# Attention scores from high and low parts: two products of 128 filled rows in place of three half-empty ones

## The reference, cut to what matters

```python
def _dilated_branch_prompt(q, k, v, window, dil):
    ...
    s = jnp.einsum('brcqhd,brckhd->brchqk', qb, kw).astype(F32) * (HEAD_DIM ** -0.5)
    ...
    p, lse = _masked_softmax(s, valid[None, None, :, None])
    o = jnp.einsum('brchqk,brckhd->brcqhd', p, vw.astype(F32))

def _combine(outs, lses):
    w = jax.nn.softmax(jnp.stack(lses, axis=0), axis=0)
    return jnp.sum(w[..., None] * jnp.stack(outs, axis=0), axis=0)
```

## Time and profile before

| | |
|---|---|
| time, median of 3 runs | 1917.29 us (1916.12 to 1919.46) |
| time of the profiled execution | 1917.52 us |
| its span, first to last instruction | 1915.7 us |
| mean granted TensorE clock | 0.937 |
| PE busy | 1698.6 us (89%) |
| DVE / ACT / POOL busy | 832.1 / 562.3 / 554.9 us |

### The profile page before, as it was taken

The page is one execution under the profiler, slowest core; times in us unless marked ns, Lnnn a source line. Parts: engine busy times, 40 slices in busy tenths (PEclk is TensorE's granted clock), DMA queues, the critical chain, the costliest instruction groups (busy, mean ns, idle before and its releaser), DMA issues. The chain is left out here.

```text
span 1915.7 us, 22177 instructions
## 1 busy us (share of the span) xinstructions
PE 1698.6 (89%) x8272; PEld 1373.3 (72%) x8272; DVE 832.1 (43%) x1552; ACT 562.3 (29%) x828; POOL 554.9 (29%) x265
## 2 busy tenths in 40 slices
PE   6999999979898688876699689999999999999983
PEld 3778888857676566655588568787878788878862
DVE  4632212046465345566556223333333333333489
ACT  4322222225555155542344221111111111111121
POOL 0233333343000035585000232222222222222354
PEclk9999999979899589986799899999999999999997
DMA  8554433451100667763142211111111111111132
GB/s 290 203 178 155 171 124 121 160 142 56 56 0 24 177 201 219 221 205 111 65 149 80 67 44 44 44 44 44 44 44 44 44 44 44 44 44 44 44 88 93
DMA packets 137588, 192.19 MB, mean 100 GB/s; under 512 B 10034, under 2 KB 86882, under 8 KB 137387
## 3 DMA queue, kind: packets, MB, share of 16 engines
q1 hardware_dynamic: 125396, 168.83, 27.9%
q10 hardware_dynamic: 12128, 22.55, 3.2%
HBM read 162.42 MB, written 28.93 MB: 100 GB/s over the span
## 5 line engine op out<-in xcount | busy, mean ns | idle before, releaser
L2420 POOL TENSOR_TENSOR mlp_w_lo<-w_room,mlp_w_hi 128x2048 fp32r<-128x2048 f32 x31 | 143.7, 4637 | 320.6 <-ACT mlp_w_hi L2416 320.5
L2721 PE MATMUL ps<-mix_hi,mlp_w_hi 128*128 128x512 f32 x512 | 206.4, 403 | 15.1 <-DVE mlp_w_lo L2420 9.6
L2619 DVE TENSOR_TENSOR x<-x,ps 128x512 f32<-128x512 f32 x224 | 154.1, 688 | 141.9 <-PE ps L2792 141.2
L2598 DVE TENSOR_TENSOR mlp_h_lo<-mlp_pos,mlp_h_hi 128x512 fp32r<-128x512 f32 x64 | 69.3, 1083 | 332.8 <-ACT mlp_h_hi L2522 330.7
L2721 PE MATMUL ps<-mix_hi,mlp_w_lo 128*128 128x512 f32 x512 | 203.2, 397 | 0.0
L2721 PE MATMUL ps<-mix_lo,mlp_w_hi 128*128 128x512 f32 x512 | 202.8, 396 | 0.0
L584 POOL TENSOR_TENSOR inp_a_lo<-inp_room,inp_a_hi 128x2048 fp32r<-128x2048 f32 x24 | 111.6, 4649 | 273.8 <-ACT inp_a_hi L718 273.8
L2792 PE MATMUL ps<-mlp_w_hi,mlp_h_hi 128*128 128x512 f32 x448 | 175.8, 392 | 5.5 <-PE ps L2727 5.1
L2792 PE MATMUL ps<-mlp_w_hi,mlp_h_lo 128*128 128x512 f32 x448 | 174.5, 389 | 0.0
L2792 PE MATMUL ps<-mlp_w_lo,mlp_h_hi 128*128 128x512 f32 x448 | 174.3, 389 | 0.0
L637 PE MATMUL ps<-inp_whi,z_hi 128*128 128x512 f32 x384 | 150.3, 391 | 2.4 <-PE ps L637 1.3
(11 more groups left out here) (375 smaller groups left out, 3512.8 us busy)
## 6 DMA issues: line engine op xcount, KB each, us to landing
w_room<-in_w_ff SPq DMA_DIRECT2D x32, 1024.0 KB, 7.0
inp_room<-in_w_ada SPq DMA_DIRECT2D x16, 1024.0 KB
proj<-inp_row ACTq DMA_DIRECT2D x54, 256.0 KB, 2.5
x<-in_cache_k SPq DMA_DIRECT2D x48, 256.0 KB, 5.0
cache_V<-in_cache_v SPq DMA_DIRECT2D x48, 256.0 KB, 4.8
x<-in_x_prompt SPq DMA_DIRECT2D x16, 512.0 KB, 9.5
inp_room<-in_w_ada_f SPq DMA_DIRECT2D x8, 1024.0 KB
x<-in_w_in ACTq DMA_DIRECT2D x16, 512.0 KB, 6.7
```

Source lines behind the costliest of these rows:

```text
L2420: pool.tensor_tensor(lo, raw, hi.bitcast(F32), ALU.subtract).then_inc(ready, 1)
L2598: dve.tensor_tensor(h_lo[s][:, j, cols], pos[u % 2][:], h_hi[s][:, j, cols].bitcast(F32), ALU.subtract).then_inc(h_ready, 1)
L2619: dve.tensor_tensor(dst, dst, ps[:, 5 + o % 3, :], ALU.add).then_inc(added, 1)
L2721: mm = pe.matmul(ps[:, u, :], w[:, k, j * P:(j + 1) * P], z[:, k, rows], start=(k == 0 and a == 0), stop=(k == KT - 1 and a == 2))
```

## The change

The keys get one tile for each head, `k_both[h]`: in the head's own 64 rows the high part, in the other 64 rows the low part. The queries keep `q_hi[h]` with zeros in the other rows and get `q_both[h]`: the low part in the own rows and a copy of the high part in the other rows. Then `q_hi x k_both` is high x high, and `q_both x k_both` is low x high + high x low in one sum over 128 rows: two products for every 512 columns instead of three.

ACT makes the high keys in two instructions of 64 rows in place of one of 128, and copies the high queries to the other rows, two new instructions of 64 rows each (`moved`). DVE makes the low keys in two instructions of 64 rows, written to the other rows. Two of the four memsets are left. ACT no longer waits for the memsets; PE does, once, and waits for the first move before `scores(0)`, for the second before unit 8.

```diff
         q_hi = [st.sb(f"qhi{h}", [P, S], F32R) for h in range(2)]
-        q_lo = [st.sb(f"qlo{h}", [P, S], F32R) for h in range(2)]
-        k_hi, k_lo = st.sb("khi", [P, S], F32R), st.sb("klo", [P, S], F32R)
+        q_both = [st.sb(f"qboth{h}", [P, S], F32R) for h in range(2)]
+        k_both = [st.sb(f"kboth{h}", [P, S], F32R) for h in range(2)]
+        OWN = [slice(HD * h, HD * (h + 1)) for h in range(2)]
+        OTHER = OWN[::-1]
...
                         if u >= 2:
                             pe.wait_ge(scored, base + u - 1)
+                        if u == TT:
+                            pe.wait_ge(moved, 2 * (2 * i + s) + 2)
...
-                            for a, (x, y) in enumerate(((q_hi, k_hi), (q_hi, k_lo), (q_lo, k_hi))):
-                                mm = pe.matmul(out, x[h][:, q * P:(q + 1) * P], y[:, c:e], start=(a == 0), stop=(a == 2))
+                            at = slice(q * P, (q + 1) * P)
+                            pe.matmul(out, q_hi[h][:, at], k_both[h][:, c:e], start=True, stop=False)
+                            mm = pe.matmul(out, q_both[h][:, at], k_both[h][:, c:e], start=False, stop=True)
...
-                    pe.wait_ge(split_done, 3 * (2 * i + s) + 3)
+                    pe.wait_ge(zeroed, 2)
+                    pe.wait_ge(split_done, 4 * (2 * i + s) + 4)
+                    pe.wait_ge(moved, 2 * (2 * i + s) + 1)
...
         def _(act):
-            act.wait_ge(zeroed, 4)
...
                     def take_keys(s):
                         act.wait_ge(turned, 2 * (2 * i + s) + 2)
-                        act.copy(k_hi[:], banks(ps, 2, 2)).then_inc(hi_done, 1)
+                        for h in range(2):
+                            act.copy(k_both[h][OWN[h], :], banks(ps, 2, 2)[OWN[h], :]).then_inc(k_hi_done, 1)
+                        for h in range(2):
+                            act.wait_ge(q_hi_done, 2 * (2 * i + s) + h + 1)
+                            act.copy(q_both[h][OTHER[h], :], q_hi[h][OWN[h], :].bitcast(F32)).then_inc(moved, 1)
...
         def _(dve):
-            for x in (q_hi, q_lo):
-                for h in range(2):
-                    rows = slice(HD * (1 - h), HD * (2 - h))
-                    dve.memset(x[h][rows, :].bitcast(F32), 0.0).then_inc(zeroed, 1)
-            dve.wait_ge(zeroed, 4)
+            for h in range(2):
+                dve.memset(q_hi[h][OTHER[h], :].bitcast(F32), 0.0).then_inc(zeroed, 1)
...
-                        dve.wait_ge(hi_done, 3 * (2 * i + s) + 3)
-                        dve.tensor_tensor(k_lo[:], banks(ps, 2, 2), k_hi[:].bitcast(F32), ALU.subtract).then_inc(split_done, 1)
+                        for h in range(2):
+                            dve.wait_ge(k_hi_done, 2 * (2 * i + s) + h + 1)
+                            dve.tensor_tensor(k_both[h][OTHER[h], :], banks(ps, 2, 2)[OWN[h], :], k_both[h][OWN[h], :].bitcast(F32),
+                                              ALU.subtract).then_inc(split_done, 1)
```

More of the change, by code:

```diff
@@ L844, in stage_prompt_attention @@
         waited = st.sb("waited", [P, 1])
-        zeroed, heads_free, turned, hi_done, split_done = (st.sem(n) for n in (
-            "zeroed", "heads_free", "turned", "hi_done", "split_done"))
+        zeroed, heads_free, turned, q_hi_done, k_hi_done, split_done, moved = (st.sem(n) for n in (
+            "zeroed", "heads_free", "turned", "q_hi_done", "k_hi_done", "split_done", "moved"))
         made, scored, neg_done, exp_done, inv_done, prob_done, prob_turned, probT_done, pv_done, mix_hi_done = (
@@ L965, in take_queries @@
                         for h in range(2):
-                            rows = slice(HD * h, HD * (h + 1))
-                            act.mul(q_hi[h][rows, :], banks(ps, 0, 2)[rows, :], SCALE).then_inc(hi_done, 1)
+                            act.mul(q_hi[h][OWN[h], :], banks(ps, 0, 2)[OWN[h], :], SCALE).then_inc(q_hi_done, 1)
                     def take_keys(s):
                         act.wait_ge(turned, 2 * (2 * i + s) + 2)
-                        act.copy(k_hi[:], banks(ps, 2, 2)).then_inc(hi_done, 1)
+                        for h in range(2):
[3 more added lines that the diff above has]
+                            act.copy(q_both[h][OTHER[h], :], q_hi[h][OWN[h], :].bitcast(F32)).then_inc(moved, 1)
                     if s == 0:
@@ L1023, in low_parts @@
                         for h in range(2):
[L1024 to L1027, removed]
+                            dve.wait_ge(q_hi_done, 2 * (2 * i + s) + h + 1)
+                            dve.scalar_tensor_tensor(out=q_both[h][OWN[h], :], in0=banks(ps, 0, 2)[OWN[h], :], scalar=SCALE,
+                                                     in1=q_hi[h][OWN[h], :].bitcast(F32), op0=ALU.mult,
                                                      op1=ALU.subtract).then_inc(split_done, 1)
-                        dve.wait_ge(hi_done, 3 * (2 * i + s) + 3)
-                        dve.tensor_tensor(k_lo[:], banks(ps, 2, 2), k_hi[:].bitcast(F32), ALU.subtract).then_inc(split_done, 1)
+                        for h in range(2):
+                            dve.wait_ge(k_hi_done, 2 * (2 * i + s) + h + 1)
+                            dve.tensor_tensor(k_both[h][OTHER[h], :], banks(ps, 2, 2)[OWN[h], :], k_both[h][OWN[h], :].bitcast(F32),
+                                              ALU.subtract).then_inc(split_done, 1)
                     if s == 0:
```

## The result

The changed kernel takes 1905.67 us (median of 8 runs, 1900.24 to 1911.94) against 1916.98 for the kernel before on the same chip: a ratio of 0.9943, 95% interval 0.9925 to 0.9961, 11.3 us faster. The forecast was 1905.6. A second measurement on another occasion gave 1906.46 and 0.9949 (0.9934 to 0.9964). The profiled execution took 1904.85 us with a span of 1903.1, 12.6 us less than before.

A forecast was written before the change was run, and what follows sets the result against it. PE's order was taken to bound the pairs, ACT/DVE chains their starts. Terms -17.6 - 2.5 + 1.2 + 5.4 + 0.8 + 1.2 - 1.4 + 1.0 = -11.9 us, from 1917.5 to 1905.6; 8-in-10 range 1899.0 to 1913.5.

The forecast's parts named there:

- Products: Prompt attention scores: 96 products removed, priced at PE's spacing, 17.6 us saved.
- the ramps: First three blocks of each pair: PE waits anyway; saving lost in second and fourth pair, +0.8 us.
- Start of the first pair: Before the first score product: queries no longer wait for memsets, DVE has one more instruction; balance -2.5 us.
- Start of the third: Third pair's start: the extra DVE instruction counts in full, ACT's extra work lies beside it; +1.2 us.
- Hand-offs: Into second and fourth pair: three more ACT instructions before the mixed-row cast delay DVE's first score; +2.7 us each, +5.4.
- Rope under the second pair: Second pair: POOL's rope rows meet two or three normalisations with less PE slack; +1.2 us (0 to 2).
- Moves: ACT's copies of high queries into the other 64 rows: about 1.02 us each; over 1.5 would refute the forecast.
- the dear moves: Rival, pair starts: eight moves at POOL's 2.36 us each, +8.4 us, time 1914.0; chance 0.14.
- POOL under the first pair: First pair: the earlier first normalisation avoids POOL's memset and meets rope rows; -1.4 us (-2.0 to 0).
- Clock: Second and fourth hand-offs: PE thinner for longer, more time at half speed; +1.0 us, bounds -2 and +3.4.
- The covered hand-off: Rival, second and fourth hand-offs: PE's two blocks of scores cover the delay, time 1899.4; chance 0.13.
- the softmax chain: Rival, whole pairs: DVE-ACT chain sets block pace, removed products become waits, time 1921.6, slower; chance 0.04.

The follow-up runs named there:

- two products and the old preparation: Kernel before without the product of high queries and low keys, all else unchanged: stage 202.74 us, time 1902.04 us, ratio 0.9909.
- the second trace of the kernel: Changed kernel profiled again on another chip, nothing edited: stage 206.98 us, ratio 0.9949.
- three products: Changed kernel with a third product per block (high queries with zeros by the keys, a second time): stage 218.20 us, time 1917.98 us, ratio 1.0005.
- without the memsets' wait: Kernel before, with PE instead of ACT waiting for the four memsets: stage 210.86 us, time 1911.44 us, ratio 0.9959.
- the reordered hand-off: Changed kernel, with ACT casting the mixed rows before moving the high queries at hand-offs inside an iteration: stage 204.57 us, time 1904.10 us, ratio 0.9926.

## Why the prediction was right, point by point

*Products.* The spacing was the right price where PE is dense, and the loss at the ramps, 0.8 us, was much too small. In the third pair, from the block of seven key blocks on, the rows of before and after say it plainly (PE's timeline, before, then after):

```profile
530.29 0.50 PE L905 MATMUL ps<-att_khi,att_qhi 128*128 128x512 f32 x1
...
566.46 0.43 PE L917 MATMUL ps<-att_probT,x 128*64 128x128 f32 x2 [0.20 <-ACT att_probT L983]
```

```profile
523.39 0.50 PE L909 MATMUL ps<-att_kboth,att_qhi 128*128 128x512 f32 x1
...
556.48 0.43 PE L922 MATMUL ps<-att_probT,x 128*64 128x128 f32 x2 [0.20 <-ACT att_probT L992]
```

36.17 us become 33.09, 3.08 less; the spacing of the products left out there gives 3.07. Before that point the six blocks should have given 1.33 and gave 0.58. With two products and the old preparation they gave nothing clear: 0.03, 0.14 and -0.10 us in the second, third and fourth pair, at 0, 2.0 and 3.1 us more at half speed. In the second pair, from the first product (464.34 in the earlier trace rows) to the seventh block, it is 10.92 before and 10.88 there (PE's timeline, before, then two products):

```profile
475.26 0.50 PE L905 MATMUL ps<-att_khi,att_qhi 128*128 128x512 f32 x1
```

```profile
458.51 0.33 PE L905 MATMUL ps<-att_khi,att_qhi 128*128 128x128 f32 x1 [2.00 <-DVE att_klo L1030]
...
469.39 0.50 PE L905 MATMUL ps<-att_khi,att_qhi 128*128 128x512 f32 x1
```

So in these runs the chain that feeds PE, and not PE, sets the time of a pair's first six blocks; the prediction had it so for three blocks, and expected two of the four pairs to get the saving back. The products are worth 3.0 to 3.2 us in each of these pairs, not 4.4.

*Start of the first pair:* -2.57 against -2.5 (-3.04 in the second trace of the kernel); the table load does stand ahead of the wait. The prediction has DVE's chain end 0.2 us behind ACT's first move; its own durations make that 0.9, and it was 1.0 (408.00 against 407.03). The forecast rests on DVE's chain, so this changes nothing in it. *Start of the third:* +1.26 against +1.2.

*Hand-offs.* Set against two products with the old preparation, they cost 3.12 and 2.60 us; with three products 3.07 and 2.90. The prediction had 2.7 for the chain. The 2.60 is the one of the four comparisons with equal time at half speed; in the others the new preparation had 3.4 us more of it. The chain is the forecast one; turning the order round gave back 2.70 us in the second pair and 0.25 in the fourth, 1.76 and 0.9 at equal time at half speed. Why the fourth gives less stays open.

*Rope under the second pair* had +1.2. From its seventh block on the second pair of the kernel after takes 31.36 us, as the fourth does, where POOL stands still; the hand-off to the second costs 0.52 more than that to the fourth, at 3.4 us more at half speed. So the runs show at most some 0.5 us of this term.

*Moves.* 1.04 us each, by the eight instructions of L980 in the kernel after; the dear moves are out.

```profile
L980 ACT CAST att_qboth<-att_qhi x8: 1041/1042/1043, 406.0 to 559.3; 64x1024 fp32r<-64x1024 f32 x8
```

*POOL under the first pair* was the weakest term, and right in its order of size by luck. I priced one wait that vanishes at -1.4. What the runs show is 2 to 3.5 us that either edit recovers alone (3.54 without the memsets' wait; the products 5.35 there against 3.0 to 3.2 in the other pairs) and both together recover once; part of this can be the clock, because the first pair of these two runs had 4.2 and 2.9 us less at half speed. In the kernel after the first normalisation does escape (0.41 us), but the third now meets the same memset:

```profile
410.26 0.41 DVE L1025 TENSOR_SCALAR att_prob<-att_prob,att_inv 128x128 f32<-128x128 f32 x1
...
412.74 0.72 POOL L239 TENSOR_TENSOR x<-att_tmp 128x256 f32<-128x256 f32 x1
...
413.10 2.32 DVE L1025 TENSOR_SCALAR att_prob<-att_prob,att_inv 128x384 f32<-128x384 f32 x1
...
413.40 1.80 POOL L1505 MEMSET q_blocks<- 128x2048 f32 x1
```

So the wait moved, which was the other end of my range. In the second trace of the same kernel it moved once more: there the fourth normalisation took 2.48 us. The Trainium skill (SBUF — State Buffer, Who interferes with whom) has the port pair held by one instruction to its end; the row agrees in that DVE ends 0.2 us behind the memset (415.42 and 415.20), but the bound I drew from the rule, one POOL instruction, doesn't hold: DVE had been waiting beside L239 since 413.10, and the memset behind that still went first. The slow normalisation of before shows the same. It began at 412.72 beside L239, 0.4 us ahead of the memset of the earlier trace rows, and ended at 414.99, 0.1 us behind it:

```profile
412.43 0.73 POOL L239 TENSOR_TENSOR x<-att_tmp 128x256 f32<-128x256 f32 x1
...
412.72 2.27 DVE L1019 TENSOR_SCALAR att_prob<-att_prob,att_inv 128x128 f32<-128x128 f32 x1
```

*Clock.* The mean over the stage went from 0.91 to 0.89, the time at half speed from 40.6 to 45.7 us: 3.4 us more in the second and in the fourth pair each, where the upper bound of the prediction had them, 3.1 less up to the end of the first pair, 1.4 more behind the last. At most half of the 5.1 us is lost, 2.5 against the +1.0 put in; the growth stays under the 7 us named as a sign of a wrong forecast. No run separates it from the ramps and the hand-offs.

*The sum.* The stage gave 10.75 of the 11.9 us, and the terms agree less well than their sum. The products with their ramps gave about 12.4 us (four times the 3.1 that two products gave in a pair) where the prediction had 17.6 - 0.8 = 16.8. Set against the same 3.1, the hand-offs cost 5.8 us with rope and clock, in place of 5.4 + 1.2 + 1.0 = 7.6; the first pair gave 2.3 beyond its products in place of 1.4, and the third 0.6 in place of nothing. So the products were booked 4.4 us too high, and the rest 3.3 us too low, which cancels most of it. The last 1.85 us of the profiled difference lie outside the stage, where nothing was changed: 2.3 less behind it, where the time at half speed fell from 188.4 to 176.8 us, and 0.4 more ahead of it. That the total agrees to 0.1 us is luck; the signs of the parts and the path at each start are what the prediction had right.

*The rivals.* The covered hand-off fell to the three-products run and to the reordered hand-off, the dear moves to L980, the softmax chain to the run with two products: it does set the pace in a pair's first six blocks, but PE's saving arrives in full as soon as these are over (3.06 to 3.09 us in the second, third and fourth pair, where the spacing gives 3.07).

## What to carry to other kernels

On a dense PE a removed product is worth its spacing, but only from the point where PE, and not the chain that feeds it, sets the pace; count each restart as a place that keeps part of the saving (here 0.8 to 1.4 us of 4.4 a pair). When a preparation grows by some instructions, follow the engine's order past them to what another engine waits for next: here the cost was not in the keys but in a cast queued behind them, and moving that cast ahead shortened both hand-offs, though not by the same. Terms that fight for the same wait don't add; measure each alone and both together before booking them twice.

## What the runs showed that was not expected

The rest of the span, which no edit touched, lay between 1693.9 us (mixed rows ahead of moves) and 1703.4 us (three products) in the ten profiles. 1.8 of these 9.5 us lie ahead of the stage, where both have 10.2 us at half speed. Behind it the longer one has more at half speed, 195.3 us against 177.9; from the next stage's first product to the end, the shorter one first:

```profile
603.90:1898.50 1294.60, 1136.57 (x5248) 923.16 (x5248) 582.35 (x985) 337.23 (x477) 402.09 (x191) 0.93 0.28 87
```

```profile
619.40:1921.60 1302.20, 1141.38 (x5248) 926.65 (x5248) 583.67 (x985) 337.06 (x477) 401.93 (x191) 0.93 0.28 87
```

The same work takes 7.6 us longer there. Single executions of the changed kernel differ by up to 12 us too (1900.24 at a mean granted clock of 0.939, 1911.94 at 0.933), so it takes no edit to move the half-speed stretches; whether a shift of the stage moves them as well isn't shown. Gains of 2 us inside a stage must be read from the trace, and with the time at half speed beside them.

A normalisation that waits for POOL can be overtaken by POOL's next instruction: 2.32 us for one that takes 0.42 elsewhere, against the at most 0.72 of the instruction it first met. In the kernel before it was 2.27 for one that takes 0.285, against 0.73.
